# Two transformer blocks on one core: second-map scaling on GpSimd and five edits of order

## What is computed

```python
def diff_attend(q, k, v, lam):
    s = jnp.einsum("bhmqd,bhmkd->bhmqk", q, k).astype(jnp.float32) * (DIFF_QK_DIM ** -0.5)
    p = jax.nn.softmax(s, axis=-1)
    w = (p[:, :, 0] - lam * p[:, :, 1]).astype(v.dtype)
    return jnp.einsum("bhqk,bhkd->bhqd", w, v)

    # mixer_stream
    gates = jax.nn.sigmoid(zgate.reshape(b, l, N_BRANCH, D_MODEL))
    ys = jnp.stack([y_four, y_conv, y_gqa, y_diff], axis=2)
    return jnp.sum(gates * ys, axis=2) @ lp["w_out"]

    # per layer
    x = x + g_m * mixer_stream(px, lp, cos, sin, ctx_kv, lam, lam_init)
    x = x + g_f * swiglu(modulate(rms_norm(x, norm_ffn[l]), sh_f, sc_f), w_ffn1[l], w_ffn3[l], w_ffn2[l])
```

## Time and profile before

| | |
|---|---|
| median of 3 runs | 2161.28 us (2160.78 to 2166.43) |
| the profiled execution: its own time | 2168.67 us |
| its span, mean granted TensorE clock | 2166.8 us, 0.946 |
| TensorE matmul busy | 1976.3 us (91%) |
| weight load, VectorE, ScalarE, GpSimd busy | 1742.4 (80%), 1018.8 (47%), 747.4 (34%), 1082.1 (50%) |
| chain that ended last: TensorE, VectorE, ScalarE | 81%, 12%, 3% |
| TensorE's longest sum of waits by line: the norms' spread L872 | 23.3 us in 6 |
| TensorE waiting for pair products L1892 | 18.7 us in 3 |

### The profile page before, as it was taken

The page is one execution under the profiler, slowest core; times in us unless marked ns, Lnnn a source line. Parts: engine busy times, 40 slices in busy tenths (PEclk is TensorE's granted clock), DMA queues, the critical chain, the costliest instruction groups (busy, mean ns, idle before and its releaser), DMA issues.

```text
span 2166.8 us, 32878 instructions
## 1 busy us (share of the span) xinstructions
PE 1976.3 (91%) x13805; PEld 1742.4 (80%) x13805; DVE 1018.8 (47%) x1690; ACT 747.4 (34%) x1208; POOL 1082.1 (50%) x565
## 2 busy tenths in 40 slices
PE   3986899988899999989988999999898998888998
PEld 3755899977798778968767888888797897888997
DVE  7853554125483576483236111112558767453114
ACT  2213254323223542262222222222243535334442
POOL 7003588746344544304333444444366751776885
PEclk9788899988899999999998999999898999998998
DMA  5344677786512214102322323322254241544552
GB/s 145 99 150 156 219 242 236 253 277 226 163 58 78 70 32 132 45 28 88 129 85 78 98 72 104 97 85 87 82 156 146 70 136 30 166 158 151 178 174 80
DMA packets 285735, 274.01 MB, mean 126 GB/s; under 512 B 6459, under 2 KB 283461, under 8 KB 285333
## 3 DMA queue, kind: packets, MB, share of 16 engines
q1 hardware_dynamic: 282164, 265.94, 38.5%
q10 hardware_dynamic: 2688, 4.86, 0.8%
q0 software_dynamic: 736, 1.12, 0.3%
HBM read 265.86 MB, written 4.19 MB: 125 GB/s over the span
## 4 chain that ended last, share of the span: by engine, by line
PE 81%; DVE 12%; ACT 3%; issue 2%; DMA 2%; POOL 1%; DVEq 0%; SPq 0%; ACTq 0%; POOLq 0%
PE gb L2290 17%; PE gb L2291 17%; PE gb L2292 17%; PE gb L1324 3%; PE gb L1325 3%; PE gb L1326 3%; PE gb L1530 3%; PE gb L1529 3%; PE gb L1528 3%; PE mb L2427 1%; PE mb L1079 1%; DVE mx L1108 1%; PE mb L611 1%; PE mb L1134 1%; POOL wl L2278 1%
## 5 line engine op out<-in xcount | busy, mean ns | idle before, releaser
L2278 POOL TENSOR_TENSOR wl<-raw,wh 128x1024 fp32r<-128x1024 f32 (+3 forms) x452 | 985.8, 2200 | 952.3 <-ACT wh L730 951.7
L730 ACT CAST wh<-raw 128x1024 fp32r<-128x1024 f32 (+3 forms) x452 | 418.7, 937 | 794.2 <-PE gb L2292 406.2
L2290 PE MATMUL gb<-xh,wh 128*128 128x256 f32 (+1 forms) x1920 | 632.9, 330 | 43.3 <-DVE pr L1892 16.0
L2291 PE MATMUL gb<-xl,wh 128*128 128x256 f32 (+1 forms) x1920 | 628.8, 327 | 0.0
L2292 PE MATMUL gb<-xh,wl 128*128 128x256 f32 (+1 forms) x1920 | 628.2, 327 | 0.0
L2290 PEld LDWEIGHTS gb<-xh,wh 128*128 128x128 f32 x1920 | 372.4, 194 | 79.8 <-issue 36.0
L2291 PEld LDWEIGHTS gb<-xl,wh 128*128 128x128 f32 x1920 | 372.4, 194 | 28.9
L2292 PEld LDWEIGHTS gb<-xh,wl 128*128 128x128 f32 x1920 | 371.7, 194 | 29.4
L1324 PE MATMUL gb<-wh,xh 128*128 128x256 f32 x608 | 174.7, 287 | 1.4 <-POOL wl L2278 1.4
L1325 PE MATMUL gb<-wh,xl 128*128 128x256 f32 x608 | 173.1, 285 | 0.0
L1326 PE MATMUL gb<-wl,xh 128*128 128x256 f32 x608 | 173.0, 284 | 0.0
(11 more groups left out here) (425 smaller groups left out, 3116.4 us busy)
## 6 DMA issues: line engine op xcount, KB each, us to landing
raw<-in_w_in SPq DMA_DIRECT2D x62, 1024.0 KB, 5.3
raw<-in_w_ada SPq DMA_DIRECT2D x48, 1024.0 KB, 6.5
raw<-in_w_ffn SPq DMA_DIRECT2D x44, 1024.0 KB, 5.1
raw<-in_mlp_w SPq DMA_DIRECT2D x32, 1024.0 KB, 6.4
raw<-in_w_ffn SPq DMA_DIRECT2D x16, 768.0 KB, 4.6
raw<-in_w_ffn SPq DMA_DIRECT2D x16, 640.0 KB, 4.2
raw<-in_ssm_w_glu SPq DMA_DIRECT2D x8, 1024.0 KB, 6.8
raw<-in_w_out SPq DMA_DIRECT2D x8, 1024.0 KB, 5.0
```

What stands on the lines that cost most here:

```text
L730: nc.scalar.copy(split_half(wh, p, j, h), raw_half(p, it, j, h)).then_inc(hi_ready, 1)
L2278: nc.gpsimd.tensor_tensor(split_half(wl, p, j, h), raw_half(p, it, j, h), split_half(wh, p, j, h).bitcast(F32), ALU.subtract)\
L2290: nc.tensor.matmul(o, H[:, k, :], XH, start=st, stop=False)
L2291: nc.tensor.matmul(o, H[:, k, :], XL, start=False, stop=False)
```

## The change

Six edits. (1) GLU runs without `lead`. (2) In GLU, MLP 2 and the last FFN phase no split is made before the squares (`split_first=False`); elsewhere the order stays. (3) Norms 0, 1, 5 and 8 use `rsqrt_beside` with its scratch in PSUM. (4) `rsqrt_beside`'s scratch is in bank 1 of gb instead of 3. (5) The first four mixed tiles go to `brh` and `brl`, one pair earlier, and w_out reads them there (`XM`). (6) GpSimd scales the second map of each differential head (`diff_pool`, between the second and the third block of branch 1 in its queue): it multiplies the reciprocal of the second sum by lambda, a 128x1 product, waits for it, and multiplies the map. VectorE computes the reciprocals ahead of the next head's row maxima and waits for GpSimd only behind them (`weighted`).

```diff
--- before.py
+++ after.py
...
         s_rc = sem("sums_inverted")
+        s_r2 = sem("pair_of_sums_inverted")
+        s_p1 = sem("second_map_scaled")
         s_go = sem("pair_output_multiplied")
...
 
-        def gemm_act(act, p, evac, before=None, tail=None):
+        def gemm_act(act, p, evac, before=None, tail=None, split_first=True):
 
             def turn(it):
                 for j in range(p.body):
                     if before is not None:
                         before(it, j)
                     nxt = ahead(p, it, j)
-                    last = tail is not None and it * p.body + j >= p.n - 2
-                    if last:
+                    i = it * p.body + j
+                    late = tail is not None and i >= p.n - 2
+                    if late:
                         evac(it, j)
-                        if it * p.body + j == p.n - 1:
+                        if i == p.n - 2 and split_first:
+                            for h in range(2):
+                                split_hi(act, nxt, h)
+                        if i == p.n - 1:
                             tail()
+                            for g in ([] if split_first else [ahead(p, it, j - 1)]) + [nxt]:
+                                if g is not None:
+                                    for h in range(2):
+                                        split_hi(act, g, h)
+                        continue
                     if nxt is not None:
                         split_hi(act, nxt, 0)
-                    if not last:
-                        evac(it, j)
+                    evac(it, j)
                     if nxt is not None:
...
 
-        def rsqrt_beside(T1, ms, y, yp, t):
+        def rsqrt_beside(T1, ms, y, yp, t, wide=None):
 
...
                 step(v.scalar_tensor_tensor(t, t, -0.5, ms, ALU.mult, ALU.mult))
+                if i == 2 and wide is not None:
+                    t, y = (a.unsqueeze(2).to_broadcast([P, a.shape[1], P]) for a in (t, y))
+                    T1.add(v.scalar_tensor_tensor(wide, t, 1.5, y, ALU.add, ALU.mult))
+                    return
                 step(v.scalar_tensor_tensor(yp if i < 2 else y, t, 1.5, y, ALU.add, ALU.mult))
...
             dve.wait_ge(s_squ, sq0[n + 1])
-            rsqrt(T1, rs[:, 0, 0:nt], rs[:, 1, 0:nt], rs[:, 2, 0:nt], rs[:, 3, 0:nt],
-                  mb[:, 0:nt, 0:1].rearrange("p a b -> p (a b)"), 1.0 / count, eps, dg[:, 0:nt, :])
+            total = mb[:, 0:nt, 0:1].rearrange("p a b -> p (a b)")
+            if n in (0, 1, 5, 8):
+                T1.add(nc.vector.tensor_scalar(rs[:, 0, 0:nt], total, 1.0 / count, eps, ALU.mult, ALU.add))
+                T1.wait()
+                rsqrt_beside(T1, rs[:, 0, 0:nt], rs[:, 1, 0:nt], *(gb[:, 1, 448 + 8 * i:448 + 8 * i + nt]
+                                                                   for i in range(2)), wide=dg[:, 0:nt, :])
+            else:
+                rsqrt(T1, rs[:, 0, 0:nt], rs[:, 1, 0:nt], rs[:, 2, 0:nt], rs[:, 3, 0:nt], total, 1.0 / count, eps,
+                      dg[:, 0:nt, :])
             T1.wait()
...
             T1.wait()
-            rsqrt_beside(T1, six[0], six[1], *(gb[:, 3, 448 + 8 * i:454 + 8 * i] for i in range(2)))
+            rsqrt_beside(T1, six[0], six[1], *(gb[:, 1, 448 + 8 * i:454 + 8 * i] for i in range(2)))
             for c in (1, 2):
...
 
+        def diff_pool(pool, l, P1):
+
+            for n in items(l, "d"):
+                c = ITEMS[n][5]
+                pool.wait_ge(s_r2, diff_index(n) + 1)
+                p1 = probs[:, (c + 1) % PROBS, 0:nk(n)]
+                P1.add(nc.gpsimd.tensor_tensor(mx[:, 2, (c + 1) % 8:(c + 1) % 8 + 1],
+                                               mx[:, 2, (c + 1) % 8:(c + 1) % 8 + 1], lamb[:, l:l + 1], ALU.mult))
+                P1.wait()
+                nc.gpsimd.tensor_tensor(p1, p1, mx[:, 2, (c + 1) % 8:(c + 1) % 8 + 1].to_broadcast([P, nk(n)]),
+                                        ALU.mult).then_inc(s_p1, 1)
+
         def grouped_pe(pe, l):
...
                 dve.wait_ge(s_ex, c + 2)
-                D1.add(v.reciprocal(mx[:, 2, c % 8:c % 8 + 2], mx[:, 1, c % 8:c % 8 + 2]))
-                D1.wait()
+                if diff_index(n) >= 4:
+                    dve.wait_ge(s_p1, diff_index(n) - 3)
+                v.reciprocal(mx[:, 2, c % 8:c % 8 + 2], mx[:, 1, c % 8:c % 8 + 2]).then_inc(s_r2, 1)
+
+            def weighted(n):
+                c = ITEMS[n][5]
                 p0, p1 = probs[:, c % PROBS, 0:nk(n)], probs[:, (c + 1) % PROBS, 0:nk(n)]
-                D1.add(v.tensor_scalar(p1, p1, mx[:, 2, (c + 1) % 8:(c + 1) % 8 + 1], lamb[:, l:l + 1],
-                                       ALU.mult, ALU.mult))
-                D1.wait()
+                dve.wait_ge(s_p1, diff_index(n) + 1)
                 v.scalar_tensor_tensor(p0, p0, mx[:, 2, c % 8:c % 8 + 1], p1, ALU.mult, ALU.add).then_inc(s_wd, 1)
 
             for i in range(len(mine) + 1):
+                if i >= 1:
+                    difference(mine[i - 1])
                 if i < len(mine):
                     for c in scores_of(mine[i]):
                         row_maximum(dve, mine[i], c)
                 if i < 2:
                     transposes_dve(dve, l, "d", 4 + 2 * i, 6 + 2 * i)
                 if i >= 1:
-                    difference(mine[i - 1])
+                    weighted(mine[i - 1])
 
...
             return lambda j, k: (xh[:, k, 0:T], xl[:, k, 0:T])
+
+        def XM(T):
+            return lambda j, k: (brh[:, k, 0:T], brl[:, k, 0:T]) if k < 4 else (xh[:, k, 0:T], xl[:, k, 0:T])
 
...
             gemm_pe(pe, q["b", 3], T, XB(T, dqTh, dqTl), branch4(pe, l, 3, lambda: back_pe(pe, l, dq)))
-            gemm_pe(pe, q["wo"], T, X2(T), first_use(pe, s_ml, 8 * l), lead=THREE)
+            gemm_pe(pe, q["wo"], T, XM(T), first_use(pe, s_ml, 8 * l), lead=THREE)
             norm_pe(pe, n0 + 2, sqr2, dg2)
...
                     act.wait_ge(s_mx, 4 * l + k // 2 + 1)
-                    nc.scalar.mul(xh[:, k, 0:T], mix[:, k, 0:T], 0.5).then_inc(s_mh, 1)
+                    nc.scalar.mul((brh if k < 4 else xh)[:, k, 0:T], mix[:, k, 0:T], 0.5).then_inc(s_mh, 1)
 
             def before(it, j):
                 if (it, j) == (0, 1):
                     back_act(act, l)
+                if (it, j) == (1, 1):
+                    mixed_hi(0, 4)
                 if (it, j) == (1, 3):
-                    mixed_hi(0, 6)
+                    mixed_hi(4, 6)
             gemm_act(act, q["b", 3], pair_tanh(act, q["b", 3], T, th2), before)
...
                 gemm_act(act, q["f2", half], lambda it, j: None,
-                         tail=(lambda: squares_act(act, n0 + 3, sqr2)) if half else None)
+                         tail=(lambda: squares_act(act, n0 + 3, sqr2)) if half else None, split_first=l < LAYERS - 1)
             act.wait_ge(s_res, 4 + l)
...
                     dve.wait_ge(s_mh, 8 * l + k + 1)
-                    v.scalar_tensor_tensor(xl[:, k, 0:T], mix[:, k, 0:T], 0.5, xh[:, k, 0:T].bitcast(F32),
+                    hi, lo = (brh, brl) if k < 4 else (xh, xl)
+                    v.scalar_tensor_tensor(lo[:, k, 0:T], mix[:, k, 0:T], 0.5, hi[:, k, 0:T].bitcast(F32),
                                            ALU.mult, ALU.subtract)\
...
                         wait_drained(dve, p, it, j, 1)
+                        if b == 3 and pair == 2:
+                            mixed_lo(0, 4)
                         if b == 3 and pair == 3:
-                            mixed_lo(0, 6)
+                            mixed_lo(4, 6)
                         multiplied(dve, p, it, j + 1)
...
             ada_copy(act, 0)
-            gemm_act(act, p_glu, pair_tanh(act, p_glu, SEQ), tail=lambda: squares_act(act, 0, sqr))
+            gemm_act(act, p_glu, pair_tanh(act, p_glu, SEQ), tail=lambda: squares_act(act, 0, sqr), split_first=False)
             act.dma_start(pnat[:, :, :], A["p"][0, 0].rearrange("(a p) d -> p a d", p=P)).then_inc(s_p, 16)
...
             ada_copy(act, 1)
-            gemm_act(act, p_m2, lambda it, j: None, tail=lambda: squares_act(act, 1, sqr))
+            gemm_act(act, p_m2, lambda it, j: None, tail=lambda: squares_act(act, 1, sqr), split_first=False)
 
...
                                     grouped_pool(pool, l)
+                                if p is L2[l]["b", 1]:
+                                    diff_pool(pool, l, P1)
                         for h in range(2):
...
                 return lambda i: ada_select(pe, group) if i == at else None
-            gemm_pe(pe, p_glu, SEQ, X, operand(0), selection(0, 0), THREE)
+            gemm_pe(pe, p_glu, SEQ, X, operand(0), selection(0, 0))
             norm_pe(pe, 0, sqr, diag, lambda: ada_block(pe, ada_tail["glu"][3]))
```

## The result

The changed kernel took **2143.39 us** (median of 6, 2133.58 to 2151.62) against 2161.03 us (median of 6, 2159.17 to 2166.43): ratio **0.9905**, 95% interval 0.9879 to 0.9930. A second set of five runs of the same kernel gave 2146.88 us against 2167.25 us, ratio 0.9905 again (0.9887 to 0.9923). The ratio of the first set is a little lower than its two medians give when divided (0.9918), so the gain is 17.6 us by those medians and some 20 us by both ratios; forecast were 22.0 us and 2139.3 us.

The account below looks back on a forecast made before the run. TensorE is busy most of the span, so only its gaps can be won. Terms sum to -22.0 us: the profiled execution goes from 2168.67 to 2146.7, the median from 2161.28 to 2139.3 us; range 2135 to 2144.

Parts of the forecast that it names:

- GLU's start: First GLU matmul waits for only the first GpSimd half, no later stall: -6.4 us, bounds -4 and -7.
- norms 0 and 1: Spread matmuls come earlier, limited by a modulation block's DMA: -1.7 us in norm 0, -3.7 in norm 1.
- branch 3 in layer 0: Four mixed steps move one pair earlier, shortening TensorE's 7.96 us wait before w_out: -4.3 us, bounds -2.5 and -6.5.
- layer 1: Mixed halves in branch 3: 8.09 us wait shortened, with a new stall of 2.4 us: -2.0 us, bounds 0 and -4.5.
- Moved at no price: The first norm's scratch in bank 1 and the splits behind the squares in GLU and MLP 2 cost nothing.
- not all heads gain: Differential heads: each layer's first four are held, 256-key heads gain only 0.06 us; layer 0 -1.4, layer 1 -0.8.
- 1 (VectorE keeps the port): Both branch-3 ends: VectorE keeps the port, -6.5 and -4.5 us, time 2134.6 us; chance 0.12.
- 2 (GpSimd's detour is longer): Differential heads: GpSimd's chain takes 2.63 us per head, about +2.5 instead of -2.2 us, time 2144; chance 0.12.
- 3 (the start is swallowed): GLU and norms arrive earlier but wait for weights; half of 14.2 us lost, time 2146.4; chance 0.09.
- 4 (row maxima blocked): Differential heads: row maxima blocked too, 3.45 us per head, 19 us more, time 2158; chance 0.02.
- 5 (TensorE at the low clock through GLU): TensorE stays at the low clock through GLU, slower than before; all fifteen other halves give 2175 us; chance 0.03.
- The reading by which moving the scaling gains nothing (2141.5): Differential heads: the engines share an SBUF read port, so the -2.2 us would be 0, time 2141.5 us.

Follow-up runs that it names:

- the second trace: Profile of the changed kernel run again without an edit, with the second set of five runs: 2146.88 us, ratio 0.9905.
- experiment 9: Changed kernel with the modulation blocks of norms 0 and 1 behind the spread matmul instead of ahead of it: 2139.35 us, ratio 0.9875.
- experiment 7: Changed kernel with the old root, all operands in SBUF, in norms 0, 1, 5 and 8; squares still first: 2153.66 us, ratio 0.9945.
- the first trace: Profile of the changed kernel from its first set of six runs, the fastest of the six; the set's median is 2143.39 us, ratio 0.9905.
- experiment 4: Changed kernel with GLU's three-half lead restored: 2155.84 us, ratio 0.9937.
- experiment 3: Kernel before the change with only the scaling of the heads' second map moved to GpSimd: 2164.10 us, ratio 0.9990.
- experiment 5: Changed kernel with the mixed halves late again, six steps ahead of pair 3's product, all into xh and xl: 2149.60 us, ratio 0.9913.
- experiment 2: Changed kernel with the scaling of the second map back on VectorE: 2147.87 us, ratio 0.9911.
- experiment 10: Changed kernel with mixed tiles spread over three pairs, modulation blocks behind the spreads, and norm 8's old root: 2136.89 us, ratio 0.9870.

## Why the prediction was right

The mechanisms named held place by place. That the sum fits as closely as it does (-22.0 against -21.9 in the second trace) is partly luck: the heads, GLU's start and norm 1 gave 3.1 us more than forecast, and some 3 us that no term had were lost behind w_out and norm 7. The medians, 17.6 to 20 us, do not tell such parts apart.

*Right as worked out:* GLU's start, with its argument that as much work as before runs at the low clock, only earlier; norms 0 and 1, both limited by the modulation block's DMA and not by the root (experiment 9 shows it); norm 5; norm 8, where the three copies cost 0.63 us (first step to spread 3.33 instead of 2.70); branch 3 in layer 0, -4.5 for -4.3; layer 1, -2.0 for -2.0, with the new stall at 1.8 to 2.0 us for 2.4 and GpSimd's third half behind it. The alternation of VectorE and GpSimd, on which three terms rested, stands in experiment 7 in its plainest form. "Moved at no price" held for the splits in GLU only together with the new root (experiment 7).

*Mis-sized:* the differential heads of layer 0, -3.1 for -1.4, of which 0.3 to 0.8 is a low-clock stretch that both traces happen to lack. The step that failed is "not all heads gain". The first heads, which I took to be held by transposes and the low clock, ran at 2.26 to 2.28 us instead of 2.63 (less the first, 3.14), and those with 256 keys at 1.59 instead of 1.71, twice the 0.06 forecast. In layer 1, -0.6 in most traces for -0.8; the -2.1 of the first trace came with a clock that did not fall there, and experiment 4's trace, with the clock low for 6.8 us instead of 3.4, gained nothing (26.77).

*Missing:* what follows a shorter wait, and what the new operand costs. Behind w_out 0.8 to 1.9 us in layer 0 and 0.8 in layer 1 are given back. The stretches of the kernel before, then of the second trace of the changed kernel (length, TensorE busy (x); the clock is the third number from the end):

```profile
1115.00:1119.00 4.00, 0.00 (x0) 0.01 (x1) 3.96 (x4) 0.00 (x0) 2.24 (x1) 0.54 0.13 18
1119.00:1122.00 3.00, 2.98 (x7) 2.42 (x8) 2.30 (x3) 1.15 (x2) 0.00 (x0) 0.50 0.93 323
1122.00:1125.00 3.00, 3.00 (x14) 2.38 (x14) 0.17 (x1) 0.00 (x0) 0.00 (x0) 0.98 0.01 2
```

```profile
1098.00:1101.00 3.00, 1.75 (x4) 1.49 (x5) 2.96 (x3) 0.00 (x0) 2.24 (x1) 0.53 0.44 156
1101.00:1105.00 4.00, 4.00 (x11) 3.02 (x11) 1.61 (x3) 1.15 (x2) 0.00 (x0) 0.50 0.81 262
1105.00:1108.00 3.00, 3.00 (x14) 2.42 (x13) 0.00 (x0) 0.00 (x0) 0.00 (x0) 1.00 0.00 0
```

Before, the low level (1.2 GHz) began in the 8 us wait and only some 7 matmuls fell into it; in the second trace of the changed kernel it begins at the end of a wait of 3.4 us and takes 15. The first 20 matmuls of w_out lose 1.2 us by that, and 0.2 in the first trace, where the clock was low for 3.4 us instead of 6.8. In GLU I had counted this, at w_out I had not.

The other 0.6 us of layer 0 are not the clock's. Edit (5) makes half of w_out's matmuls read `brh` and `brl`, and twelve of those take 2.80 us at full clock where twelve on `xh` and `xl` take 2.72 (TensorE; the kernel before, then the second trace of the changed kernel):

```profile
1142.38 0.39 PE L2290 MATMUL gb<-xh,wh 128*128 128x512 f32 x1
...
1145.10 0.39 PE L2290 MATMUL gb<-xh,wh 128*128 128x512 f32 x1
```

```profile
1124.08 0.40 PE L2337 MATMUL gb<-brh,wh 128*128 128x512 f32 x1
...
1126.88 0.39 PE L2337 MATMUL gb<-xh,wh 128*128 128x512 f32 x1
```

That is 0.234 us per matmul instead of 0.227, in all nine traces with the edit. In the kernel before and in experiments 3 and 5, w_out has 0.227 throughout, while branch 1, whose operand is `brh` and `brl` in every kernel, has 0.234. In layer 1, with 256 columns, w_out shows no such difference. Why the two buffers differ is not shown.

*Rivals:* 1 (VectorE keeps the port) fell, the steps alternate; 2 (GpSimd's detour is longer) fell, 2.38 us per head and 0.19 for the small product; 3 (the start is swallowed) fell by experiment 4; 4 (row maxima blocked) fell, 0.64 each; 5 (TensorE at the low clock through GLU) fell, the high level came within 5 us of the first matmul. The reading by which moving the scaling gains nothing (2141.5) fell by experiments 2 and 3.

*Norm 8's segment* is 0.6 us longer than the three copies explain. That 0.6 us lies in the 100 matmuls behind norm 7's spread (16.33 us before, 16.94 and 16.99 in the two traces of the changed kernel): the clock came back to its high level 6.3 us behind that spread before, and 7.6 to 7.8 us behind it in both traces of the changed kernel. In experiment 10, where the old root is back and these matmuls take 16.52, the segment is 1.1 us shorter.

*Open:* the segment behind norm 5 (127.04 us before and in experiment 3, 127.33 with the old roots) is 125.5 to 126.5 in all traces with the new root, because a low-clock stretch at the same matmul is missing; no run tells why.

## What to carry to other kernels

Where VectorE's short steps take as long as GpSimd's current instruction, look at their operands: one of them in PSUM cost a copy of 0.2 us per Newton step and saved 2.1 us per blocked step (2.27 to 0.17), and moving blocked steps ahead of a product that nobody waits for yet saved 4.5 us in layer 0; in layer 1 two at a time were better than four. Measure the matmuls again when their operand moves to another buffer: here that cost 0.6 us. After a wait has been shortened, ask what now ends last, here a DMA for work that had no need to come first (4.6 us), and how much of the low clock that was hidden in the wait falls on the work behind it. Edits of 1 to 4 us are read from segments between the same two instructions, not from spans, since here an untouched prologue alone moved by 12 us.

## What was not expected

The changed kernel's runs spread over 18 us in the first set and 2 in the second, those of the kernel before over 7 and 15. The stretches at the low clock between the same matmuls come and go from one execution to the next: a head of layer 1 took 2.53 us in one trace and 3.94 to 4.01 in all others with the scaling on GpSimd.
